# Pairs of experts i and i + 8 with 32 shared slots, as a third product beside two

## The reference, cut to what matters

```python
def moe_ffn(x, router_w, router_b, w_gate, w_up, w_down):   # 16 experts in 4 groups of 4
    probs = jax.nn.softmax((xt @ router_w), axis=-1)
    sel = probs + router_b
    gscore = lax.top_k(sel.reshape(-1, N_GROUPS, EXPERTS_PER_GROUP), TOP_K)[0].sum(-1)
    gbest = jnp.argmax(gscore, axis=-1)                      # the best group
    _, idx = lax.top_k(jnp.where(in_group, sel, -jnp.inf), TOP_K)   # two experts in it
    gates = probs at idx, divided by their sum
    h = silu(xt @ w_gate[e]) * (xt @ w_up[e])                # 1024 -> 512
    return sum over the two experts of gate * (h @ w_down[e])  # 512 -> 1024
```

## Time and profile before

| | |
|---|---|
| median of 3 runs | 769.87 us (769.69 to 771.09) |
| profiled execution | 769.16 us, span 767.3 us |
| TensorE busy | 743.0 us (97%), granted clock 0.994 |
| VectorE, ScalarE, GpSimd busy | 296.0, 241.7, 105.4 us |
| moved by DMA | 246.13 MB, mean 321 GB/s |

### The profile page before, as it was taken

How to read it: one execution, slowest core, us unless ns; L and a number is a source line. 1 busy time by engine, 2 the same in 40 slices (tenths; PEclk the granted TensorE clock), 3 DMA queues, 4 the chain that set the end, 5 groups by cost and what they waited for, 6 DMA issues and landing times.

```text
span 767.3 us, 10640 instructions
## 1 busy us (share of the span) xinstructions
PE 743.0 (97%) x4092; PEld 440.9 (57%) x4093; DVE 296.0 (39%) x537; ACT 241.7 (32%) x454; POOL 105.4 (14%) x68
## 2 busy tenths in 40 slices
PE   9999999999999899999999999999999999999993
PEld 6989887645353353353799888645353454335332
DVE  5589927642111111120667656742111111112115
ACT  5556366242111111120735666332111111112112
POOL 2013000067000000002041000066000000000022
PEclk9999999999999999999999999999999999999997
DMA  9998333889999999999995433789999999995311
GB/s 327 297 390 308 118 110 131 290 354 423 419 422 422 422 422 421 422 422 415 387 389 209 136 139 137 286 361 423 420 422 422 421 422 422 421 422 202 146 55 55
DMA packets 51430, 246.13 MB, mean 321 GB/s; under 512 B 6249, under 2 KB 6466, under 8 KB 26818
## 3 DMA queue, kind: packets, MB, share of 16 engines
q1 hardware_dynamic: 50818, 243.55, 79.9%
q10 hardware_dynamic: 576, 2.10, 1.0%
HBM read 244.58 MB, written 1.05 MB: 320 GB/s over the span
## 4 chain that ended last, share of the span: by engine, by line
PE 82%; DMA 13%; DVE 3%; ACT 1%; issue 1%; SPq 0%; DVEq 0%; ACTq 0%
PE ps L1905 22%; PE ps L1705 14%; PE ps L1917 13%; DMA ring<-in_moe_w_down 12%; PE ps L1700 12%; PE ps L1872 3%; PE ps L1891 3%; PE ps L1956 2%; PE ps L1667 1%; PE ps L1880 1%; PE ps L1988 1%; DMA ring<-in_a_w_in 1%; PE ps L1640 1%; PE ps L1742 1%; PE ps L1661 1%; PE ps L2038 1%
## 5 line engine op out<-in xcount | busy, mean ns | idle before, releaser
L1905 PE MATMUL ps<-ring,scratch 128*64 128x512 f32 x640 | 140.3, 592 | 0.1
L1917 PE MATMUL ps<-ring,scratch 128*64 128x512 f32 x512 | 114.5, 596 | 8.2 <-DMA ring<-in_moe_w_down 8.2
L1905 PEld LDWEIGHTS ps<-ring,scratch 128*64 128x64 f32 x640 | 48.3, 137 | 88.3 <-issue 88.0
L1096 DVE TENSOR_TENSOR ring_lo<-ring,w_hi 128x2048 fp32r<-128x2048 f32 x36 | 83.4, 2331 | 18.3 <-ACT w_hi L728 17.1
L677 POOL TENSOR_TENSOR scratch<-rounded,gate 128x256 f32<-128x256 f32 x16 | 14.1, 884 | 492.8 <-PE ps L2046 309.0
L1917 PEld LDWEIGHTS ps<-ring,scratch 128*64 128x64 f32 x512 | 36.7, 137 | 74.6 <-issue 72.1
L728 ACT ACTIVATE w_hi<-ring 128x2048 fp32r<-128x2048 f32 x35 | 66.7, 1913 | 27.9 <-PE ps L1705 15.7
L1508 DVE TENSOR_TENSOR scratch<-ps,scratch 128x512 f32<-128x512 f32 x16 | 11.1, 692 | 157.1 <-PE ps L1905 157.0
L1519 DVE SCALAR_TENSOR_TENSOR rounded<-ps,gslot,rounded 128x512 fp32r<-128x512 f32 x32 | 24.0, 751 | 106.1 <-ACT rounded L972 106.1
L1905 PE MATMUL ps<-spare,scratch 128*64 128x512 f32 x256 | 56.3, 592 | 0.0
L972 ACT ACTIVATE rounded<-ps,gslot 128x512 fp32r<-128x512 f32 x32 | 22.0, 688 | 99.0 <-PE ps L1917 99.0
(11 more groups left out here) (299 smaller groups left out, 1069.0 us busy)
## 6 DMA issues: line engine op xcount, KB each, us to landing
ring<-in_moe_w_down SPq DMA_DIRECT2D x64, 1024.0 KB, 15.0
ring<-in_moe_w_up SPq DMA_DIRECT2D x48, 1024.0 KB, 14.6
ring<-in_moe_w_gate SPq DMA_DIRECT2D x32, 1024.0 KB, 12.2
spare<-in_moe_w_gate SPq DMA_DIRECT2D x32, 1024.0 KB, 14.9
ring<-in_a_w_in SPq DMA_DIRECT2D x16, 1024.0 KB, 13.2
scratch<-in_moe_w_up SPq DMA_DIRECT2D x16, 1024.0 KB, 19.7
ring<-in_kv_w SPq DMA_DIRECT2D x8, 1024.0 KB, 14.7
ring<-in_a_w_out SPq DMA_DIRECT2D x4, 1024.0 KB, 14.2
```

The source lines that it names most:

```text
L1096: V.tensor_tensor(ring_lo[:, piece_slot(i), :, :], ring[:, piece_slot(i), :, :], w_hi[:, i % HI, :, :].bitcast(F32), ALU.subtract).then_in ...
L1905: last = mm(ps[half, bank, :], xe[:, HALF_K * part + k, own], weight(odd, matrix, part, e)[:, k, :], start=part == 0 and k == 0, stop=part ...
L1917: last = mm(ps[half, bank, :], hT[:, 2 * part + k, half], weight(odd, DOWN, part, e)[:, 2 * k + cols, :], start=part == 0 and k == 0, stop ...
```

## The change

A pair is now experts i and i + 8, which never stand in one group. Its 128 slots are four quarters of 32. The second expert has quarters 2 and 3 (rows 64 to 127), the first has quarter 1 (rows 32 to 63), and quarter 0 goes to the first expert, or to the second where that has more than 64 tokens and the first at most 32 (`second`, one integer for each pair from 1 on; pair 0 never shares). Each step of k has three matmuls: quarter 0 with the weights of whoever has it, whose place is computed from a register (`weight_of`), quarter 1 with those of the first, and rows 64 to 127 with those of the second. `share_out` on VectorE lays the slots and gates out by quarters. The overflow round stays for what is left.

Besides this, the buffers are placed anew; `TWICE` is 7, so that one more chunk of the next pair has a second place (`last_place`, where v and xn lay and lie); SyncE issues the second places' chunks between the ring's last ones and ahead of ln1's factors, which ScalarE's queue loaded before; the first piece comes in two halves of k; the first layer norm's outputs come in halves; fillers are fewer; the zeroing of ys and put in `route` is replaced by plain semaphore steps, and the first even pair of a stage no longer adds up; one step of the reciprocal root goes; and the last layer norm is cut into other parts.

```diff
-TWICE = 6
+TWICE = 7
+SHARE = 32
-TURN_BANKS = (0, 1, BANK_C, BANK_D)
+TURN_BANKS = (BANK_C, BANK_D, 0, 1)
...
+        def chunk_places(layer, odd, c):
+            if odd and c == SPARE:
+                return scratch, *LATE
+            first, other = ((RING + min(i, SPARE) if odd and i < TWICE else chunk_slot(layer, i)) * CHUNK_SIZE
+                            for i in (c, c + 1))
+            return weights[:, :, :, :].rearrange("p s k n -> p (s k n)"), first, other
...
+                if i == 0:
+                    sp.dma_start(ring[:, 0, 0:2, :], w[:, 0:2, :]).then_inc(w_first_in, 16)
+                    sp.dma_start(ring[:, 0, 2:4, :], w[:, 2:4, :]).then_inc(arrive[0], 16)
+                    return
...
-            FIRST = ((GATE, 0), (GATE, 1), (UP, 0))
-            REST = ((UP, 1), (DOWN, 0), (DOWN, 1))
+            BOTH = (0, 1)
+            FIRST = ((GATE, 0, BOTH), (GATE, 1, BOTH), (UP, 0, BOTH), (UP, 1, (0,)))
+            REST = ((UP, 1, (1,)), (DOWN, 0, BOTH), (DOWN, 1, BOTH))
...
             def normalise(i):
-                nc.scalar.activation(x[:, 1, :], ps[:, 2:4, :].rearrange("p b n -> p (b n)"), ACT.Identity,
-                                     scale=rs[:, 2, 1:2], bias=rs[:, 4, 1:2]).then_inc(x_done[1], 1)
+                for half in range(2):
+                    nc.scalar.activation(x[:, 1, half * COLS:(half + 1) * COLS], ps[:, 2 + half, :], ACT.Identity,
+                                         scale=rs[:, 2, 1:2], bias=rs[:, 4, 1:2]).then_inc(x_half[1], 1)
...
+            act.wait_ge(w_first_in, 16)
+            nc.scalar.activation(w_hi[:, 0, 0:2, :], ring[:, 0, 0:2, :], ACT.Copy).then_inc(w_first, 1)
...
                         if part == 0:
                             act.wait_ge(gslot_ready, pair + 1)
+                            act.wait_ge(x_affine, 2 * layer + 1)
...
+                step(V.tensor_scalar(second_f[:, 1:PAIRS], ps[:, BANK_B, N + PAIRS + 1:N + E], float(SLOTS), None, ALU.is_gt))
+                step(V.scalar_tensor_tensor(second_f[:, 1:PAIRS], ps[:, BANK_B, N + 1:N + PAIRS], SHARE + 0.5,
+                                            second_f[:, 1:PAIRS], ALU.is_lt, ALU.mult))
+                V.tensor_copy(second[0:1, 1:PAIRS], second_f[0:1, 1:PAIRS])
+                V.tensor_copy(count_f[0:1, 0, 0:PAIRS], ps[0:1, BANK_B, N:N + PAIRS])
+                step(V.scalar_tensor_tensor(count_f[0:1, 0, PAIRS:E], second_f[0:1, 0:PAIRS], -float(SHARE),
+                                            ps[0:1, BANK_B, N + PAIRS:N + E], ALU.mult, ALU.add))
...
+                def weight_of(who, odd, matrix, part, k):
+                    home, first, other = chunk_places(layer, odd, chunk_of(matrix, part, 0))
+                    return home[:, bass.ds(who * (other - first) + first + k * COLS, COLS)]
...
+                rows_of = (slice(0, SHARE), slice(SHARE, 2 * SHARE), slice(SLOTS, 2 * SLOTS))
...
                         for k in range(HALF_K):
-                            for e in range(2):
-                                half = slice(e * SLOTS, (e + 1) * SLOTS)
-                                own = slice((2 - 2 * odd + e) * SLOTS, (3 - 2 * odd + e) * SLOTS)
-                                last = mm(ps[half, bank, :], xe[:, HALF_K * part + k, own], weight(odd, matrix, part, e)[:, k, :],
+                            for rows, w in zip(rows_of, (weight_of(who, odd, matrix, part, k),
+                                                         weight(odd, matrix, part, 0)[:, k, :],
+                                                         weight(odd, matrix, part, 1)[:, k, :])):
+                                last = mm(ps[rows, bank, :], own[:, HALF_K * part + k, rows], w,
                                           start=part == 0 and k == 0, stop=part == 1 and k == HALF_K - 1)
...
+                    who = pe.value_load(second[0:1, bass.ds(i, 1)], min_val=0, max_val=1)
+                    into_hidden(BANK_A, two, odd, GATE, gate_ps, who)
...
-                    if not odd:
-                        add_up(0)
-                    add_up(1).then_inc(acc_ps, 1)
+                    if odd:
+                        add_up(1)
+                    else:
+                        with pe.If(two > 0):
+                            add_up(0)
+                            add_up(1)
...
-            for _ in range(2):
-                nothing(BANK_A)
-            for _ in range(40):
+            for _ in range(36):
                 nothing(BANK_A, COLS // 2)
             turn_normed()
...
-            for _ in range(7):
-                nothing(BANK_A)
+            for _ in range(6):
+                nothing(BANK_A, COLS // 2)
```

More of the change, by code:

```diff
@@ L1 @@
+import itertools
 import math
@@ L195, in build @@
         chunks = sb("chunks", [1, PAIRS], I32)
-        xn = at(0, TT, D)
-        both_late = at(0, 2, HALF_K, COLS)
-        late = [both_late[:, e, :, :] for e in range(2)]
+        xn = v
+        LATE = (0, 46 * K)
+        late = [at(first, HALF_K, COLS) for first in LATE] + [last_place]
         xr_lo = x_lo[:, :, :].rearrange("p k t -> p (k t)").rearrange("p (t n) -> p t n", t=TT)
-        place = [16 * K]
+        place = [8 * K]
         def carve(*shape, parts=P, home=scratch):
@@ L294, in build @@
         x_done = [sem(f"x_done{t}") for t in range(TT)]
+        x_half = [sem(f"x_half{t}") for t in range(TT)]
+        gates_ready = sem("gates_ready")
         xn_step = sem("xn_step")
@@ L937, in moe @@
                 act.wait_ge(router_in, ROUTER)
-                act.wait_ge(routed, layer + 1)
-                for half in range(2):
-                    nc.scalar.activation(ys_hi[:, half * COLS:(half + 1) * COLS], seg[:, :], ACT.Copy, scale=0.0
-                                         ).then_inc(ys_act, 1)
+                act.sem_inc(ys_act, 2)
                 take_xe(xc_ps, layer + 1, BANK_C, range(0, 4), columns_of(0))
-                act.wait_ge(x_done[0], 2 * layer + 1)
-                act.wait_ge(x_done[1], 2 * layer + 1)
+                act.wait_ge(x_done[0], 2 * layer + 2)
+                act.wait_ge(x_done[1], 2 * layer + 2)
                 nc.scalar.activation(xr_hi.rearrange("p t n -> p (t n)"), xn.rearrange("p t n -> p (t n)"),
@@ L996, in _ @@
             second_parts(0)
+            normalise_for_experts(0, 0, 0)
             router_exp(0)
-            normalise_for_experts(0)
+            normalise_for_experts(0, 0, 1)
+            for half in range(2):
+                normalise_for_experts(0, 1, half)
             moe(0)
@@ L1077, in _ @@
             second_parts(1)
+            normalise_for_experts(2, 0, 0)
             router_exp(1)
-            normalise_for_experts(2)
+            normalise_for_experts(2, 0, 1)
+            for half in range(2):
+                normalise_for_experts(2, 1, half)
             moe(1)
@@ L1688, in piece @@
                         pe.wait_ge(lo_ready, i + 1)
-                    for j in range(2):
-                        if i == number == 0 and j == 1:
-                            pe.wait_ge(hi_ready, 1)
+                    if i == number == 0:
+                        for ks in (range(2), range(2, HALF_K)):
+                            if ks.start:
+                                pe.wait_ge(hi_ready, 1)
+                            for j, c, k in itertools.product(range(2), range(2), ks):
+                                mm(ps[:, 4 + j, c * T:(c + 1) * T], w[:, k, (2 * j + c) * P:(2 * j + c + 1) * P], xs[:, k, :],
+                                   start=c == 0 and k == 0, stop=k == HALF_K - 1, skip_group_check=True)
+                    for j in range(0 if i == number == 0 else 2):
                         bank = 4 + 2 * (n % 2) + j
```

312 lines of the change are left out of this document (182 added, 130 removed).

## The result

The changed kernel takes 1144.8 us (median; 1144.25 to 1145.13), the kernel before 770.25 us in the same job: a ratio of 1.4861, 95% interval 1.4837 to 1.4884. The forecast of 726 us, its range and its sign were wrong. Rival 1, *width changes drain*, priced at 1180 us with a chance of 0.14, is what happened.

The account below looks back on a forecast made before the run. DMA was taken to bound the MoE stages to pair 4, then TensorE's chain, tied with DMA. Terms -39.8 - 0.8 - 0.6 - 1.5 - 0.4 = -43.1 us, from 769.16, gave 726 us; range 718 to 764.

Parts of the forecast that it names:

- Rival 1: MoE product steps: changing matmul width drains TensorE, 1.21 us more a step in all 16 pairs; 1180 us, chance 0.14.
- The three products: MoE product steps: two 32-column matmuls and one of 64 run side by side, step stays 0.86 us; 0.
- cheaper form: MoE product steps: widths only exclude each other, switching free, 20.6 us a pair; 1046 us, within the 0.14 for draining.
- 0.18 us a pair: MoE pairs: extra time that still fits under DMA's 29.8 us, so only six pairs pay (26 us).
- about 0.23 us a step: MoE product steps: extra time from which the width-change loss was said to decide the outcome.
- The rounds that go away: Second MoE stage, pairs 6 and 7: both overflow rounds vanish, 91.04 us becomes 51.29; -39.8 us.
- start: Kernel start: half of the first megabyte is enough and one filler goes, w_hi ready earlier; -0.6 us.
- between stages: Between the MoE stages: halves let x be turned earlier, and fillers take 0.65 instead of 1.5 us; -1.5 us.
- the end: Last VectorE operations: one of 0.74 us moves into the wait for ACT's root, 0.3 us doesn't fit; -0.4 us.
- one more chunk ahead: Weight stream of both MoE stages: 19 chunks prefetched instead of 18, fewer small DMA waits; -0.8 us in all.
- Registers: MoE product steps: register addresses and the load of `second` stay hidden behind the array; 0.
- rival 3: MoE pairs: sequencer time a step, or the unhidden load of `second`, shows; +5 to +22 us, 731 to 750, chance 0.08.

Follow-up runs that it names:

- the kernel without jump: Changed kernel with the wide product cut in two of 32 columns (four products a step) and TensorE's overflow-round code removed: 724.98 us, ratio 0.9419.
- the first experiment: Changed kernel with the wide product of each step cut in two of 32 columns, so four products of one width; overflow code kept: 732.26 us, ratio 0.9533.
- the third experiment: Changed kernel with the sharing condition never met and two products of 64 columns a step, so overflow rounds come back: 765.63 us, ratio 0.9948.

## Why the prediction was wrong

- **The failed step is "The three products", taken at 0**, that is, a step of 0.86 us. It measured 1.985 us: +1.127 us, times 24 steps 27.0 us a pair. Sixteen pairs are 433 us; from the 725.0 of the kernel without jump, less its 9.2 us of DMA waits, that gives 1149, measured 1144.8. By the rows of whole pairs, (31.83 - 13.92) + (15.95 - 7.07) = 26.8 us a pair, it is 1144.4.
- **Where the reading went astray.** The earlier trace rows are two tiles of 64 side by side, a couple every 0.43 us, four tiles of 32: in their single records four start within 20 ns and the next four 109 ns later, and a matmul of 128 columns alone has that pace too, 0.11 us. I read "disjoint tiles stream at once" out of them, but what they show is "disjoint tiles *of one width* stream at once". The only row with two widths, showed a price, and I set it aside because its tiles overlap. The price came with disjoint tiles as well, 0.27 us for two changes against the 0.35 of the earlier trace rows. In the changed kernel's trace a change is 0.134 us, and 32 and 64 columns don't overlap in the step of 1.985 us.
- **The rival's size.** The bound from the earlier trace rows had 0.35 us for two changes, measured 0.27: 24 x 0.08 x 16 = 31 us, nearly all of 1180 less 1145. The DMA waits that it took off, some 5 us a stage, were 8.2 us in both stages together. Its cheaper form, widths that only exclude each other with free switching, 1046 us, is out: sorting by width changed neither columns nor overlap and gave back 69 us, which free switching would not.
- **Also of rival 1, right:** every pair pays, since 27 us is far above the 4.2 us a pair (29.8 less 25.6, 0.18 us a step) that fit under DMA, and the DMA waits vanish. The prediction's "0.18 us a pair" is that price of a step, and its "about 0.23 us a step" doesn't come out of its rows.
- **The rounds that go away, right.** No lines of them after; pairs 6 and 7 take 50.84 us in both stages of the first experiment. Between no sharing (765.6) and sharing without a jump (725.0) lie -40.6 us; forecast -39.8. With the jump it is -33.4.
- **The small terms:** start and between stages as forecast; the end gave 1.05 instead of 0.4; one more chunk ahead gave nothing measurable instead of 0.8. Together -2.8 us of span in the third experiment, against a forecast of -3.3.
- **Registers, 0: right** for the step. Of rival 3, the bare load never showed. What did show was not per step: it was the idle time behind the jump over the overflow code, +7.3 us (732.3 less 725.0). It stands in the kernels with four products in a step of 0.86 us, and in none with two or three, though these jump over the same code; why, no run shows. No term and no rival had it.

## What to carry to other kernels

Tiles side by side on TensorE paid here only where all had the same width (32 with 32, 64 with 64, each product 128 rows and 512 moving columns): 0.86 us a step, and 1.985 with both widths. If the work falls into parts of 32 and 64 columns, cut the 64 in two of 32: twice the instructions, nothing lost in a step of 0.86 us. If widths must be mixed, sort by width; that took 69 of some 420 us back here.

When rows support "these things run side by side", write down in what the rows are all alike (here the width) before using them for a case in which they aren't. A change that rests on one such step deserves a kernel with that step alone, like the three products in the kernel before.

Idle time with "issue" in the first turn of a long loop, behind code that is jumped over, is worth looking up in the DMA view by packets of instructions. That one is there says little, since kernels without the idle time have them too; that one starts the same time ahead of each end of the idle time says more. The test is to take the skipped code out.

## What was unexpected of the hardware

- 32-column and 64-column tiles on disjoint columns did not overlap in three kernels (the changed one, the one sorted by width, the kernel before with three products): a step of alternating widths takes 1.985 us, of which 0.27 are the two changes. Four 32-column products with two kinds of operand addresses take 0.86 us.
- Jumps over skipped code in the first turn of a loop left TensorE idle for 0.6 to 4.7 us in the kernels with four products a step. It went on 2.71 to 3.00 us after a 16 KB packet of instructions had started, and the granted clock was 0.79 in 174 to 182 us, behind an idle time of 3.8 us. In the same place without the jump: none. The first experiment's later turns of the first loop, 230 to 370 us, were free of both the idle time and such packets. Why the same jump left no such idle time with two or three products a step, no run shows.
- 128 never executed instructions moved one such idle time from 4.06 to 1.04 us; with 64 or 192 it stayed at 3.79 and 3.77.
